# A fused decoder layer on one core: turns, scores and values grouped in even slots, adaLN products moved

## The chip, the core and the metric

The kernel runs on one core of a Trainium2 chip. The metric is the device time of one execution in microseconds (us), the median of several runs. The engines are TensorE (PE, and PEld for its weight loads), VectorE (DVE), ScalarE (ACT), GpSimd (POOL) and SyncE (SP), which issues the transfers. Each engine works through its own list of instructions in order; semaphores tie them together.

## The reference

One layer of a hybrid decoder for a prompt of 512 tokens and 8 single sample tokens, width 1024, 8 + 8 heads of 64:

```
mod = silu(c) @ w_ada + b_ada                      # 6 x 1024 numbers: shift, scale, gate, twice
h   = rms_norm(x, g_norm1) * (1 + scale1) + shift1
z   = h @ w_in                                     # q, k, v of mixers A and B, indexer, gates
A   : index scores -> top 128 keys -> softmax(q k - alibi) v
B   : softmax(q k + forget sums) v
x  += gate1 * ((sigmoid(ga) * (A @ w_o_a) + sigmoid(gb) * (B @ w_o_b)) @ w_out)
x  += gate2 * (relu(h2 @ w_up)^2 @ w_down)         # h2 from norm 2, shift2, scale2
```

The sample tokens do the same against paged caches of 256 rows.

## The kernel before

Projections are products in which both the weights and the input are split into a high and a low part: `half_tile` does three products per chunk of 128 inputs (hi x hi, lines 976; hi x lo, 977; lo x hi, 978), for one half of the columns (256 or 264 of the 520). A half tile over all 8 chunks is 24 products, over 4 chunks 12. ScalarE rounds the weights (`round_w`, line 1499), GpSimd or VectorE makes the rest (`rest_w`).

The stretch that the change touches is the loop over `ITERATIONS`: steps p = 0 to 9 with slots s = 0 to 7. Every engine goes through the same (p, s) list with its own work for each, and this fixes the order. Step p projects the q, k, v of head pair p (slots 0 to 3 one half tile of 24 products each, slots 4 to 7 half of one, 12 products), and does the attention of pair p - 1, in 8 units: U = 8 (p - 1) + s. A unit is one head and one block of 128 queries; block qb = 0 to 3 sees (qb + 1) x 128 keys. In step 0 index scores (line 1128) stand in that place. Its work for a unit:

- `scores(U)`, at even U for two heads at once: products of 64 rows, into banks 4 and 5 (L1064);
- `logits(U)` on VectorE adds the mask or forget sums and takes the maximum, `exps(U)` on ScalarE (L1550), `inverse_sum(U)` on VectorE and `probs(U)` on ScalarE (L1556) a slot later;
- `turn_probs(U)`: qb + 1 transpositions into bank 6 (L1073), at slot U + 2, and `store_pt(U)` on ScalarE copies them out (L1563);
- `values(U)` for two heads, products of 64 columns into bank 7 (L1087), at slot U + 5;
- `round_o` on ScalarE and `rest_o` on VectorE (L2095) split the finished output of a pair, in slots 3 and 4.

The projected q and k go through `to_tokens` (four transpositions into bank 2, L1105), `square_tok` (ScalarE), `mean_squares` (VectorE, L2072, L2073), `power` (GpSimd, L829), `normalize` (VectorE, L2082) and `to_features` (four transpositions into bank 3, L1118), for q at slots 2 to 4 and for k at slots 4 to 6; `store_back` takes them out of bank 3.

Two kinds of other work lie in the same slots. `side_step` prepares the samples (list `SIDE`), alternately in banks 2 and 3; ScalarE's `side_store` empties the bank in the slot after. The adaLN products: the last 8 blocks of 512 columns of `w_ada` are each done in two halves, at the 16 places of `ADA_AT`. `mod_part(h)` does one half, 8 products of 32 columns into bank 3 (L1043), `mod_rows_part` (ScalarE, L1606) copies the block out, `mod_turn_part` (L1049) brings it to features by multiplying with `fold_p`, a matrix that also adds the four partial sums, and `mod_add_part` (VectorE) adds the bias. The weights come by `load_part(h)`, issued by SyncE in the slot after half h - 2, when that is done. `mod_part` of an even h waits until the block before is added, and until the side work of earlier steps has left bank 3:

```
            elif h % 2 == 0:
                pe.wait_ge(mod_ready, ADA_BLOCKS + h // 2)
                pe.wait_ge(back_read, 2 * p)
                before = sum(at[0] < p for at in SIDE)
                if before:
                    pe.wait_ge(side_read, before)
```

After the loop come the last gates, the output projections and the MLP.

Of the kernel before, what the change touches and what calls it, by code (L numbers as in the profile page):

```python
# [15 lines left out]
ALU = mybir.AluOpType  # L16
ACT = mybir.ActivationFunctionType
F32 = mybir.dt.float32
# [4 lines left out]
P = 128  # L23
# [37 lines left out]
SPL = 2  # L61
ADA_BLOCKS = 4
ADA_ORDER = [0, 2, 1, 3] + list(range(4, 12))
ADA_AT = [(p, s) for p in range(6) for s in range(0 if p in (1, 4) else 2, 4)]
N_H = NCH + 2
KEPT = list(range(T_WO + NCH + SPL, T_MLP)) + [T_MLP + 2, T_MLP + 3]
N_KEPT = NCH - SPL
# [39 lines left out]
def split_at(p, s):  # L107

    q, t = slot_before(p, s)
    return [T_PAIR + 3 * q + HALVES_AT.index(t) // 2 + SPL] if 0 <= q <= N_PAIRS + 1 and t in HALVES_AT[1::2] else []  # L110
# [36 lines left out]
def layer(nc, a):  # L147
    ctx = ExitStack()
    with ctx:
# [7 lines left out]
        def sb(name, shape, dt=F32, at=None):  # L157
            size = int(np.prod(shape[1:])) * 4
            size += -size % 32
            if at is None:  # L160
                at = place["at"]
                place["at"] += size
            return nc.alloc_sbuf_tensor_at(name, list(shape), dt, offset=at), at, at + size

        def new(name, shape, dt=F32):
            return sb(name, shape, dt)[0]
# [18 lines left out]
        rs8 = new("rs8", [P, 8])  # L185
        neghalf = new("neghalf", [P, 8])
        sm_tok_s = new("sm_tok_s", [NS, P])
        page_row = new("page_row", [1, NS * NPAGE], I32)

        x_t = new("x_t", [P, NCH, T])  # L190
# [111 lines left out]
        rs_all = sb("rs_all", [P, T], F32, h_hi_at + 4 * T * 4)[0]  # L302
        mod_row, _, e1 = sb("mod_row", [P, 2, SEQ], F32, ts_at)
        cond_p, _, e2 = sb("cond_p", [P, NCH, 32], F32, ts_at + 2048)
        fold_p, _, e2 = sb("fold_p", [P, 9], F32, e2)
        assert e2 <= e1
        part = [sb(f"part{j}", [P, 2, SEQ], F32, at)[0] for j, at in enumerate((pad_at, padb_at, padb_at + 4096, e1))]
        nrm0, _, e1 = sb("nrm0", [P, 2, SEQ], F32, e1)
# [188 lines left out]
            return (qb + 1) * P  # L497


        ITERATIONS = [(p, s) for p in range(N_PAIRS + 1) for s in range(SLOTS)] + [(N_PAIRS + 1, s) for s in range(5)]  # L500
        N_UNITS = N_PAIRS * 2 * QB
        SAMPLE_POWERS = [(5, 7), (6, 1), (8, 2), (8, 4)]
        K_BACK = 6
# [257 lines left out]
        def _(pool):  # L761
# [57 lines left out]
            pool.wait_ge(gq_consts, 1)  # L819
            pool.wait_ge(h_hi_ready, N_H)  # L820
            pool.wait_ge(h_lo_ready, N_H)
            pool.tensor_copy(cond_p[:, :, :], cond_t[:, :, :])
            pool.tensor_copy(fold_p[:, :], fold[:, :]).then_inc(cond_kept, 1)

            def power(n):
                pool.wait_ge(ms_tok, n + 1)
# [51 lines left out]
        def _(pe):  # L878
# [167 lines left out]
            def mod_turn_part(n):  # L1046
                pe.wait_ge(mod_row_ready, ADA_BLOCKS + n + 1)
                for q in range(4):
                    last = mm(bank[3][:, 9 * q:9 * q + 9], mod_row[:, 0, q * P:(q + 1) * P], fold_p[:, :], start=True, stop=True)  # L1049
                last.then_inc(mod_turned, 1)  # L1050

            def unit(U):
# [127 lines left out]

            for p, s in ITERATIONS:
                U = SLOTS * (p - 1) + s
                if s < 4:
                    project(T_PAIR + 3 * p + HALVES_AT.index(s) // 2, HALVES_AT.index(s) % 2)
                elif p <= N_PAIRS:
                    if s in FIRST_HALF_AT:
                        project(T_PAIR + 3 * p + 2, FIRST_HALF_AT.index(s), range(4))
                    else:
                        project(T_PAIR + 3 * p + 2, HALVES_AT.index(s) % 2, range(4, NCH))
                if (p, s) in ADA_AT:  # L1190
                    mod_part(ADA_AT.index((p, s)))
                if p < N_PAIRS:
                    if s == 2:
                        to_tokens(p, 0)
                    if s == 4:
                        to_tokens(p, 1)
                        to_features(p, 0)
                    if s == K_BACK:
                        to_features(p, 1)
                if s == 0 and 1 <= p <= N_PAIRS:  # L1200
                    to_tokens(p - 1, 2)
                if p == 0:
                    if s == 0:
                        pe.wait_ge(act_evac, act_evac_value(T_PAIR - 1, 1))
                        pe.wait_ge(sm_ready, 3)
                    for n in range(3 * s + s % 2, 3 * s + 3, 2):
                        index_scores(n)
                if 0 <= U - 2 < N_UNITS:
                    turn_probs(U - 2)
                if 0 <= U < N_UNITS and U % 2 == 0:  # L1210
                    if U == 0:
                        pe.wait_ge(idx_relu, 24)
                    scores(U)
                if 0 <= U - 5 < N_UNITS and U % 2:
                    values(U - 5)
                if (p, s) == slot_before(*SIDE[4]):
                    first_samples(p)
                if (p, s) in SIDE:
                    side_step(SIDE.index((p, s)))
                if (p, s) in ADA_AT[1::2]:  # L1220
                    mod_turn_part(ADA_AT.index((p, s)) // 2)
# [193 lines left out]
        def _(act):  # L1415
# [229 lines left out]

            for p, s in ITERATIONS:
                U = SLOTS * (p - 1) + s
                before = slot_before(p, s)
                if before in SIDE:
                    side_store(SIDE.index(before))  # L1650
                for i in split_at(p, s):
                    round_w(i)
                if s in HALVES_AT and (p, s) < (N_PAIRS + 1, 4):
                    kd, half = divmod(HALVES_AT.index(s), 2)
                    if p < N_PAIRS:
                        store_z(p, kd, half)
                    else:
                        store_gate(3 * (p - N_PAIRS) + kd, half)
                if p < N_PAIRS and s in (2, 4):
                    square_tok(p, s // 2 - 1)  # L1660
                if (p, s) in ADA_AT[1::2]:
                    mod_rows_part(ADA_AT.index((p, s)) // 2)
                if p == 0:
                    for n in range(3 * s, 3 * s + 3):
                        relu_scores(n)
                if 0 <= U - 2 < N_UNITS:
                    store_pt(U - 2)
                if 0 <= U - 1 < N_UNITS:
                    probs(U - 1)
                if 0 <= U < N_UNITS:  # L1670
                    exps(U)
                if s == 3 and p >= 2:
                    round_o(p - 2)
                if p < N_PAIRS:
                    if s == 4:
                        store_back(p, 0)
                    if s == K_BACK:
                        store_back(p, 1)
                if s == 0 and 1 <= p <= N_PAIRS:
                    store_v(p - 1)  # L1680

# [141 lines left out]
        def _(dve):  # L1823
# [75 lines left out]
            def mod_add_part(n):  # L1899
                at = slice(4 * ADA_ORDER[ADA_BLOCKS + n], 4 * ADA_ORDER[ADA_BLOCKS + n] + 4)  # L1900
                dve.wait_ge(mod_turned, ADA_BLOCKS + n + 1)
                dve.tensor_tensor(mod_t[:, at, :], bank[3][:, 0:36].rearrange("p (q c) -> p q c", c=9),
                                  vec_t[:, at].unsqueeze(2).to_broadcast([P, 4, 9]), ALU.add).then_inc(mod_ready, 1)

            def rest_h(src, j, value):
# [300 lines left out]
            for p, s in ITERATIONS:  # L2206
# [14 lines left out]
                    dve.wait_ge(masks_made, 2 * p)  # L2221
                if 0 <= U - 1 < N_UNITS:
                    inverse_sum(U - 1)
                if s == 4 and p >= 2:
                    rest_o(p - 2)
                if p < N_PAIRS:
                    if s in (2, 4):
# [284 lines left out]
```

## Time and profile before

| | |
|---|---|
| median of 3 runs | 942.34 us (941.03 to 943.38) |
| profiled execution | 939.24 us, span of its instructions 937.4 us |
| TensorE busy | 919.6 us, 98% of the span |
| VectorE, ScalarE, GpSimd busy | 493.9, 396.2, 141.0 us |
| granted TensorE clock | 1.00 |
| chain that ended last | 88% TensorE, 5% VectorE, 4% issue, 2% ScalarE |
| steps 1 to 8 of the loop | from 105.7 to 372 us |

A busy share of TensorE counts pipelined instructions from start to end, so it overlaps: two products that start 0.12 us apart last 0.28 us each. Start times tell more than durations. Slot (3, 1) means step 3, slot 1. "Idle before" is the time in which an engine had nothing under way, with the instruction that ended it.

### The profile page before, as it was taken

To read this page: it belongs to the slowest core of one execution; us is meant where nothing else is said; L and a number is where in the kernel's file an instruction comes from. 1 tells how busy PE (TensorE), PEld (TensorE's weight loads), DVE (VectorE), ACT (ScalarE), POOL (GpSimd) and SP (SyncE) were. 2 spreads that over 40 slices of the span, in tenths; PEclk is the share of its full clock that TensorE was granted. 3 is DMA by queue.
4 is the path that set the end of the run, shared out by engine and by line. 5 is a ranking of instruction groups with operands and counts; after the bars stand their busy time and mean duration, and the time that the engine had idled before them with its cause. 6 is when DMAs were issued, how large, how long until landed. Compare 5 with 4: busy or idle time off the path is not lost.

```text
span 937.4 us, 19878 instructions
## 1 busy us (share of the span) xinstructions
PE 919.6 (98%) x7554; PEld 847.5 (90%) x7554; DVE 493.9 (53%) x1178; ACT 396.2 (42%) x829; POOL 141.0 (15%) x140
## 2 busy tenths in 40 slices
PE   8999999999999999999999999999999999999997
PEld 7797678777878878998999999999999999999997
DVE  3654778864645797731277576444333344443332
ACT  3354646654756667233334244333111244431121
POOL 4200233232236674300000000000000000000000
PEclk9999999999999999999999999999999999999999
DMA  9648765256325554977233431233333333333312
GB/s 319 219 117 235 188 214 174 71 169 193 110 64 158 163 183 131 279 251 249 69 91 97 129 90 47 69 92 94 98 96 91 90 90 89 89 89 90 89 45 92
DMA packets 176233, 124.54 MB, mean 133 GB/s; under 512 B 14739, under 2 KB 152019, under 8 KB 176164
## 3 DMA queue, kind: packets, MB, share of 16 engines
q1 hardware_dynamic: 176034, 123.50, 43.6%
q8 instruction: 45, 0.74, 0.3%
q14 instruction: 24, 0.20, 0.1%
q10 hardware_dynamic: 130, 0.10, 0.0%
HBM read 116.99 MB, written 6.59 MB: 132 GB/s over the span
## 4 chain that ended last, share of the span: by engine, by line
PE 88%; DVE 5%; issue 4%; ACT 2%; POOL 1%; POOLq 0%; ACTq 0%; DVEq 0%
PE bank L976 24%; PE bank L977 23%; PE bank L978 23%; PE bank L1064 2%; PE bank L1087 2%; PE bank L1043 2%; PE bank L882 2%; PE bank L1073 2%; PE bank L1105 1%; PE bank L1261 1%; PE bank L900 1%; PE bank L1049 1%; PE bank L1128 1%; DVE sel L2027 1%; PE bank L1118 1%
## 5 line engine op out<-in xcount | busy, mean ns | idle before, releaser
L976 PE MATMUL bank<-h_hi,w_hi 128*128 128x256 f32 (+1 forms) x1232 | 357.5, 290 | 1.2 <-issue 0.6
L977 PE MATMUL bank<-h_lo,w_hi 128*128 128x256 f32 (+1 forms) x1232 | 348.0, 282 | 0.0
L978 PE MATMUL bank<-h_hi,w_lo 128*128 128x256 f32 (+1 forms) x1232 | 347.5, 282 | 0.0
L976 PEld LDWEIGHTS bank<-h_hi,w_hi 128*128 128x128 f32 x1232 | 232.3, 189 | 23.5 <-issue 17.0
L977 PEld LDWEIGHTS bank<-h_lo,w_hi 128*128 128x128 f32 x1232 | 232.1, 188 | 0.0
L978 PEld LDWEIGHTS bank<-h_hi,w_lo 128*128 128x128 f32 x1232 | 231.7, 188 | 0.0
L976 PE MATMUL bank<-u_hi,w_hi 128*128 128x264 f32 (+1 forms) x512 | 145.1, 283 | 0.0
L977 PE MATMUL bank<-u_lo,w_hi 128*128 128x264 f32 (+1 forms) x512 | 144.7, 283 | 0.0
L978 PE MATMUL bank<-u_hi,w_lo 128*128 128x264 f32 (+1 forms) x512 | 144.5, 282 | 0.0
L2444 DVE TENSOR_TENSOR w_lo<-raw,w_hi 128x1024 fp32r<-128x1024 f32 x58 | 71.1, 1225 | 132.9 <-ACT w_hi L1783 132.9
L1783 ACT ACTIVATE w_hi<-raw 128x1024 fp32r<-128x1024 f32 x58 | 61.3, 1056 | 139.8 <-PE bank L978 139.8
L976 PEld LDWEIGHTS bank<-u_hi,w_hi 128*128 128x128 f32 x512 | 96.6, 189 | 0.0
L977 PEld LDWEIGHTS bank<-u_lo,w_hi 128*128 128x128 f32 x512 | 96.4, 188 | 0.0
L978 PEld LDWEIGHTS bank<-u_hi,w_lo 128*128 128x128 f32 x512 | 96.3, 188 | 0.0
L835 POOL TENSOR_TENSOR w_lo<-raw,w_hi 128x1024 fp32r<-128x1024 f32 x27 | 64.6, 2391 | 134.0 <-ACT w_hi L1499 93.0
L1974 DVE TENSOR_TENSOR w_lo<-raw,w_hi 128x1024 fp32r<-128x1024 f32 x32 | 39.3, 1227 | 52.2 <-ACT w_hi L1499 52.1
L1499 ACT ACTIVATE w_hi<-raw 128x1024 fp32r<-128x1024 f32 x59 | 62.2, 1054 | 7.9 <-PE bank L978 7.8
L1790 ACT ACTIVATE u_f<-bank 128x256 f32<-128x256 f32 (+1 forms) x56 | 21.8, 389 | 97.2 <-PE bank L978 92.3
L2453 DVE TENSOR_TENSOR u_f<-u_f 128x256 f32<-128x256 f32 (+1 forms) x56 | 24.0, 429 | 71.2 <-ACT u_f L1790 70.8
L1550 ACT ACTIVATE lg<-lg,stat 128x128 f32<-128x128 f32 (+3 forms) x64 | 35.9, 560 | 33.4 <-DVE stat L2064 33.0
L1556 ACT ACTIVATE lg<-lg,stat 128x128 f32<-128x128 f32 (+3 forms) x64 | 35.9, 561 | 13.3 <-DVE stat L2068 13.3
L976 PE MATMUL bank<-h_hi,kept_hi 128*128 128x256 f32 (+1 forms) x128 | 36.5, 285 | 0.1
(330 smaller groups left out, 1372.2 us busy)
## 6 DMA issues: line engine op xcount, KB each, us to landing
raw<-in_w_in SPq DMA_DIRECT2D x44, 512.0 KB, 4.0
part<-in_w_ada SPq DMA_DIRECT2D x32, 512.0 KB, 5.5
raw<-in_w_up SPq DMA_DIRECT2D x32, 512.0 KB, 4.1
raw<-in_w_down SPq DMA_DIRECT2D x32, 512.0 KB, 4.0
ada<-in_w_ada SPq DMA_DIRECT2D x4, 2048.0 KB, 13.6
kv<-in_cache_k_b SPq DMA_DIRECT2D x16, 256.0 KB, 4.1
qbc<-q_d SPq DMA_DIRECT2D x16, 256.0 KB, 4.6
kv<-in_cache_k_a SPq DMA_DIRECT2D x16, 256.0 KB, 4.5
```

Of the source, the lines that this page charges most:

```text
L835: pool.tensor_tensor(parts(i)[1], raw[:, i % RAW], parts(i)[0].bitcast(F32), ALU.subtract).then_inc(lo_ready, 1)
L976: mm(out, hi[:, k, :], x_h, start=first and k == ks[0], stop=False)
L977: mm(out, hi[:, k, :], x_l, start=False, stop=False)
L978: end = mm(out, lo[:, k, :], x_h, start=False, stop=last and k == ks[-1])
L1499: A(parts(i)[0], raw[:, i % RAW], ACT.Copy).then_inc(hi_ready, 1)
L1550: A(lg[:, U % 3, 0:w], lg[:, U % 3, 0:w], ACT.Exp, bias=stat[:, 8 + U % 8:9 + U % 8], scale=unit_slope(U), accum_out=stat[:, 16 + U % 8:17 ...
L1556: A(lg[:, U % 3, 0:w], lg[:, U % 3, 0:w], ACT.Copy, scale=stat[:, 26 + U % 2:27 + U % 2]).then_inc(p_ready, 1)
L1783: A(w_hi[:, i % SPL], raw[:, i % RAW], ACT.Copy).then_inc(hi_ready, 1)
L1790: A(u_f[:, 2 * (b % 2) + half, 0:CUT[half + 1] - CUT[half]], half_bank(half + 4 * ((T_MLP + b) % 2), half), ACT.Relu).then_inc(act_evac, 1)
L1974: dve.tensor_tensor(parts(i)[1], raw[:, i % RAW], parts(i)[0].bitcast(F32), ALU.subtract).then_inc(lo_ready, 1)
L2444: dve.tensor_tensor(w_lo[:, i % SPL], raw[:, i % RAW], w_hi[:, i % SPL].bitcast(F32), ALU.subtract).then_inc(lo_ready, 1)
L2453: dve.tensor_tensor(uf, uf, uf, ALU.mult).then_inc(u_sq, 1)
```

## The change

TensorE's odd slots keep the projection and side work alone. In even slots stand, in this order, the turn of the odd unit U - 3, `to_features` (slots 4 and 6), `scores(U)`, `values(U - 6)` and the turn of the even unit U - 2; ScalarE's stores follow that order. `round_o` and `rest_o` come a slot later, and the loop gets one more slot, (9, 5). In steps 2, 3 and 5 the adaLN halves move from slots 2 and 3 to slots 0 and 1. Odd halves come ahead of the projection of their slot. The block is turned by four transpositions instead of products with `fold_p`, and VectorE adds the four partial sums (`tensor_reduce`).

```
-ADA_AT = [(p, s) for p in range(6) for s in range(0 if p in (1, 4) else 2, 4)]
+ADA_AT = [(p, s) for p in range(6) for s in (range(4) if p in (1, 4) else (0, 1) if p else (2, 3))]
...
-                    last = mm(bank[3][:, 9 * q:9 * q + 9], mod_row[:, 0, q * P:(q + 1) * P], fold_p[:, :], start=True, stop=True)
+                    last = tr(bank[3][:, q * P:(q + 1) * P], mod_row[:, 0, q * P:(q + 1) * P], ident[:, :])
...
+                if (p, s) in ADA_AT[1::2]:
+                    mod_part(ADA_AT.index((p, s)))
                 if s < 4:
                     project(T_PAIR + 3 * p + HALVES_AT.index(s) // 2, HALVES_AT.index(s) % 2)
...
-                if (p, s) in ADA_AT:
+                if (p, s) in ADA_AT[0::2]:
                     mod_part(ADA_AT.index((p, s)))
...
-                        to_features(p, 0)
-                    if s == K_BACK:
-                        to_features(p, 1)
...
-                if 0 <= U - 2 < N_UNITS:
-                    turn_probs(U - 2)
-                if 0 <= U < N_UNITS and U % 2 == 0:
-                    if U == 0:
-                        pe.wait_ge(idx_relu, 24)
-                    scores(U)
-                if 0 <= U - 5 < N_UNITS and U % 2:
-                    values(U - 5)
+                if U % 2 == 0:
+                    if 0 <= U - 3 < N_UNITS:
+                        turn_probs(U - 3)
+                    if p < N_PAIRS and s in (4, K_BACK):
+                        to_features(p, s // 2 - 2)
+                    if 0 <= U < N_UNITS:
+                        if U == 0:
+                            pe.wait_ge(idx_relu, 24)
+                        scores(U)
+                    if 0 <= U - 6 < N_UNITS:
+                        values(U - 6)
+                    if 0 <= U - 2 < N_UNITS:
+                        turn_probs(U - 2)
...
+                if (p, s) in ADA_AT[1::2]:
+                    mod_rows_part(ADA_AT.index((p, s)) // 2)
                 for i in split_at(p, s):
                     round_w(i)
...
-                if 0 <= U - 2 < N_UNITS:
+                if U % 2 == 0 and 0 <= U - 3 < N_UNITS:
+                    store_pt(U - 3)
+                if p < N_PAIRS and s in (4, K_BACK):
+                    store_back(p, s // 2 - 2)
+                if U % 2 == 0 and 0 <= U - 2 < N_UNITS:
                     store_pt(U - 2)
...
-                if s == 3 and p >= 2:
+                if s == 4 and p >= 2:
                     round_o(p - 2)
...
+                link(dve.tensor_reduce(mod_sum[:, :, :], bank[3][:, :].rearrange("p (q j c) -> p q c j", q=4, j=4)[:, :, 0:9, :],
+                                       AX_X, ALU.add))
+                dve.tensor_tensor(mod_t[:, at, :], mod_sum[:, :, :],
...
-                if s == 4 and p >= 2:
+                if s == 5 and p >= 2:
                     rest_o(p - 2)
```

## Rows read from the trace of the kernel before

**Rows 1.** Windows: stretch, us; busy us (instructions) by engine; clock, DMA share, GB/s

```profile
core 0: us, PE busy (x) PEld busy (x) DVE busy (x) ACT busy (x) POOL busy (x), PEclk, DMA share, GB/s
130.90:148.00 17.10, 16.41 (x128) 13.69 (x129) 16.45 (x59) 11.16 (x26) 2.51 (x3) 1.00 0.28 82
164.80:183.00 18.20, 17.48 (x136) 14.66 (x136) 17.49 (x58) 11.17 (x26) 2.45 (x3) 1.00 0.25 76
...
105.70:372.00 266.30, 260.57 (x2130) 215.08 (x2129) 184.70 (x597) 167.01 (x412) 106.81 (x52) 1.00 0.49 150
```

**Rows 2.** Timeline of TensorE, steps 6 and 7: start us, us, instruction, idle before

```profile
310.17 0.60 PE L1166 MATMUL bank<-ident,z_s 128*8 128x128 f32 x4
310.52 0.36 PE L976 MATMUL bank<-h_hi,w_hi 128*128 128x256 f32 x1
310.72 0.28 PE L977 MATMUL bank<-h_lo,w_hi 128*128 128x256 f32 x1
...
313.44 0.60 PE L1105 MATMUL bank<-ident,z 128*128 128x128 f32 x4
313.88 0.60 PE L1073 MATMUL bank<-ident,lg 128*128 128x128 f32 x4
314.41 0.49 PE L1064 MATMUL bank<-k_fm,q_fm 64*128 64x128 f32 x4
314.83 0.39 PE L976 MATMUL bank<-h_hi,w_hi 128*128 128x264 f32 x1
315.06 0.28 PE L977 MATMUL bank<-h_lo,w_hi 128*128 128x264 f32 x1
...
317.84 0.60 PE L1073 MATMUL bank<-ident,lg 128*128 128x128 f32 x4
318.37 0.88 PE L1087 MATMUL bank<-p_t,v_tok 128*64 128x128 f32 x12
319.17 0.38 PE L976 MATMUL bank<-h_hi,w_hi 128*128 128x256 f32 x1
319.39 0.28 PE L977 MATMUL bank<-h_lo,w_hi 128*128 128x256 f32 x1
```

**Rows 3.** Timeline of TensorE: an adaLN block is turned, slot (5, 3)

```profile
267.48 1.06 PE L1049 MATMUL bank<-fold_p,mod_row 128*128 128x9 f32 x8
```

**Rows 4.** Timeline of TensorE: index scores behind adaLN products, scores behind turns

```profile
88.44 0.92 PE L1128 MATMUL bank<-ki,q_idx 64*128 64x384 f32 x4
...
300.72 0.92 PE L1064 MATMUL bank<-k_fm,q_fm 64*128 64x384 f32 x4
```

**Rows 5.** What TensorE waited for: us in total, times, longest

```profile
PE bank L1049 <- ACT mod_row L1606: 1.2, 2, 0.7
PE bank L1073 <- ACT lg L1556: 0.8, 1, 0.8
...
PE bank L1154 <- issue: 0.6, 1, 0.6
...
PE bank L1154 <- ACT k_fm L1581: 0.5, 1, 0.5
```

**Rows 6.** Timeline of TensorE, slot (0, 6)

```profile
100.53 0.66 PE L1118 MATMUL bank<-ident,tok 128*128 128x128 f32 x4 [1.25 <-DVE tok L2082]
```

**Rows 7.** Timeline of TensorE: first and third adaLN half of step 1

```profile
108.75 1.07 PE L1043 MATMUL bank<-part,cond_p 128*32 128x512 f32 x8
...
119.56 1.50 PE L1043 MATMUL bank<-part,cond_p 128*32 128x512 f32 x8
```

**Rows 8.** Timeline of ScalarE: the side store at the start of step 3

```profile
178.38 0.58 ACT L1612 ACTIVATE ki_pt<-bank 128x512 f32<-128x512 f32 x1
```

**Rows 9.** Timelines of VectorE and TensorE in step 4: normalize, to_features

```profile
242.00 0.69 DVE L2082 TENSOR_TENSOR tok<-bank,rs 128x512 f32<-128x512 f32 x1
...
243.27 0.60 PE L1118 MATMUL bank<-ident,tok 128*128 128x128 f32 x4
```

**Rows 10.** Timelines of GpSimd and VectorE, slot (7, 4)

```profile
331.21 2.38 POOL L835 TENSOR_TENSOR w_lo<-raw,w_hi 128x1024 fp32r<-128x1024 f32 x1
...
331.52 2.09 DVE L2073 TENSOR_SCALAR ms<-ms 128x8 f32<-128x8 f32 x1
```

More of the change, by code:

```diff
@@ L187, in layer @@
         sm_tok_s = new("sm_tok_s", [NS, P])
+        mod_sum = new("mod_sum", [P, 4, 9])
         page_row = new("page_row", [1, NS * NPAGE], I32)
@@ L304, in layer @@
         cond_p, _, e2 = sb("cond_p", [P, NCH, 32], F32, ts_at + 2048)
-        fold_p, _, e2 = sb("fold_p", [P, 9], F32, e2)
         assert e2 <= e1
@@ L497, in width @@
             return (qb + 1) * P
-        ITERATIONS = [(p, s) for p in range(N_PAIRS + 1) for s in range(SLOTS)] + [(N_PAIRS + 1, s) for s in range(5)]
+        ITERATIONS = [(p, s) for p in range(N_PAIRS + 1) for s in range(SLOTS)] + [(N_PAIRS + 1, s) for s in range(6)]
         N_UNITS = N_PAIRS * 2 * QB
@@ L821, in _ @@
             pool.wait_ge(h_lo_ready, N_H)
-            pool.tensor_copy(cond_p[:, :, :], cond_t[:, :, :])
-            pool.tensor_copy(fold_p[:, :], fold[:, :]).then_inc(cond_kept, 1)
+            pool.tensor_copy(cond_p[:, :, :], cond_t[:, :, :]).then_inc(cond_kept, 1)
             def power(n):
@@ L1660, in _ @@
                     square_tok(p, s // 2 - 1)
-                if (p, s) in ADA_AT[1::2]:
-                    mod_rows_part(ADA_AT.index((p, s)) // 2)
                 if p == 0:
@@ L1671, in _ @@
                     exps(U)
-                if s == 3 and p >= 2:
+                if s == 4 and p >= 2:
                     round_o(p - 2)
[L1674 to L1678, printed above, removed]
                 if s == 0 and 1 <= p <= N_PAIRS:
@@ L1901, in mod_add_part @@
                 dve.wait_ge(mod_turned, ADA_BLOCKS + n + 1)
-                dve.tensor_tensor(mod_t[:, at, :], bank[3][:, 0:36].rearrange("p (q c) -> p q c", c=9),
+                link(dve.tensor_reduce(mod_sum[:, :, :], bank[3][:, :].rearrange("p (q j c) -> p q c j", q=4, j=4)[:, :, 0:9, :],
+                                       AX_X, ALU.add))
+                dve.tensor_tensor(mod_t[:, at, :], mod_sum[:, :, :],
                                   vec_t[:, at].unsqueeze(2).to_broadcast([P, 4, 9]), ALU.add).then_inc(mod_ready, 1)
```

## The prediction

> **What bounds the kernel now.** I read the page first, then the windows by step, the timeline of TensorE for one clean step and one step with adaLN work, the list of what TensorE waited for, and last the timelines of VectorE, ScalarE and GpSimd around those waits. In the pair loop (steps 1 to 8) the reader is to see TensorE busy for 260.6 of 266.3 us at a granted clock of 1.00 [rows 1]. So only some 6 us there are open waits; everything else that can be won on TensorE must come from a denser instruction stream. The two stretches in the same rows say the opposite of another engine: from the middle of step 1 to step 2, and from the middle of step 2 to step 3, VectorE is busy for 16.45 of 17.10 and 17.49 of 18.20 us, 96% both times. There VectorE sets the pace and TensorE waits for what it hands on.
>
> The dense stream is not smooth. The rhythm of the projection is 2.78 us over 23 products, 0.121 each (315.06 to 317.84) [rows 2]. Four transpositions take 0.44 (313.44 to 313.88), 0.11 each. But the four turns that come ahead of scores or of values take 0.53, and the first product of a projection after scores or values takes 0.23 or 0.22 to the next instead of 0.12. A projection that follows transpositions pays nothing: four of them in 0.35 and a first product of 0.20, together 0.55, are 4 x 0.11 + 0.12 within 0.01 [rows 2]. The price stands where full-array work meets the scores (64 rows) or the values (64 columns): about 0.09 on the way in, 0.10 on the way out.
>
> **What the grouping saves on TensorE.** Per pair of slots the order was projection, turns, scores, projection, turns, values. It becomes turns, scores, values, turns, and two projection halves in a row.
> - Out of scores: 27 of the 32 score blocks are followed by a projection now, and will be by values: 27 x 0.10 = 2.7 us. The other 5 are followed by side work.
> - Out of values: 19 of 32 are followed by a projection (the others by side or adaLN work), and will be by turns: 1.9 us.
> - Into values: 32 x 0.09 = 2.9 us, since values will stand behind scores, if scores to values costs nothing of its own. The trace has no such pair. The nearest is the index scores straight behind the adaLN products: a block 64x384 lasts 0.92 there, and 0.92 behind turns [rows 4], so the switch is paid once however it is entered. I take 0; the other end is a full price of 0.10 x 32 = 3.2 us less gain. The Trainium skill (TensorE: Matmul & The Clock Gate, Part 3, The mechanism) says that a weight load overlaps running products only if their row groups differ; scores and values share rows, so by that rule the 3.2 would be lost. No row here shows that pair.
> - adaLN: each of 8 blocks is turned by 8 products in 1.06 us [rows 3] and will be by 4 transpositions in 0.60 [rows 2]: 8 x 0.46 = 3.7. The switch behind them, 0.08 x 8 = 0.6, goes; the odd half pays 0.05 more, because it goes straight into a projection: -0.4. Together 3.9.
>
> Sum 11.4 us. VectorE gets one small reduction (144 numbers a partition) for each of the 8 blocks, in the slot after a projection half; I cost it at nothing, hidden by TensorE's next half of 24 x 0.121 = 2.9 us. Without that cover it could not be worth more than one pass of 512 columns each, 0.69 [rows 9].
>
> **Waits that go.** The waits for the adaLN row (1.2), for a turn at (3, 1) (0.8) and before the side transpositions at (1, 7) and (2, 7) (0.6 and 0.5) [rows 5] have their cause removed: the odd half comes a projection earlier, the turn at an odd slot is gone, and store_back comes ahead of the exponentials. In step 0 the 1.25 us before to_features [rows 6] is covered by index scores that now come first. That is 4.3 us of idle time; each of the six costs some 0.14 more, because work that is resumed starts with an emptied pipeline (four transpositions last 0.60, but what follows starts after 0.44 [rows 2]): 5.1 us.
>
> **Waits that come.** Here the change takes back.
> - Loads of w_ada in step 1. Of the four half blocks the third lasts 1.50 instead of 1.07: its weights are not there at once. They are asked for when the first is done, and that stays. From the end of the first (109.8) to the start of the third (119.6) lie 9.8 us [rows 7], afterwards 8.2 (two projection halves of 2.9, the second half block 1.0, transpositions and scores 1.4). So the wait grows from 0.4 to 2.0. The same for the fourth block, whose loads queue behind a store of v: I put 1.6. Together 3.2 us: step 1 gains nothing up to its middle.
> - Side stores. mod_part in slot 0 of steps 2, 3 and 5 must wait until bank 3 is emptied by the side_store of slot 7, and that stands on ScalarE behind the exponential of slot 7, which waits for VectorE. In step 3 that store ends at 178.96 [rows 8], about when the projection of (3, 0) was over; adaLN work came two slots later and never saw this. VectorE's chain is full, and rest_o (one pass of 512 columns, nearest row 0.69 [rows 9]) moves into it, from a slot where it was hidden. TensorE gets there up to 1.3 us earlier, the store comes 0.7 later: 2.0 us. Step 2 the same without rest_o but with all of the time saved before: 2.0. Step 5, where VectorE has slack, 0.4. Together 4.4.
> - to_features and scores of slot 6. rest_o now stands between inverse_sum and normalize in slot 5, and waits for round_o, which ScalarE does behind the exponential of slot 4, itself behind the second turn. In step 4 normalize ends at 242.69 and to_features starts at 243.27 [rows 9]: 0.58 to spare. The chain grows by 0.69 and about 0.7 of waiting for round_o, TensorE comes 0.4 later: 0.2 of wait, and logits in front of the next scores bring it to 0.6 to 1.0. If the mean's small operation meets GpSimd's rest_w it gets worse: 8 columns took 2.09 us and ended with GpSimd's pass (331.21 + 2.38) [rows 10]. I put 0.6, 0.7, 1.0, 1.0, 0.5, 0.5, 0.5, 0.4 for steps 1 to 8: 5.2 us. The Trainium skill (SBUF - State Buffer, two separate sides) calls the pair of ports that these two share an exclusive lock, held for the whole instruction; this row agrees (2.09 us).
>
> Sum 12.8 us.
>
> **The total.** -11.4 - 5.1 + 12.8 = -3.7 us. The profiled execution took 939.24 us (span 937.4); 935.5 after. The median is 942.34, so 938.6 by the median. All terms lie in steps 0 to 8; nothing behind them is touched, except that values(62), round_o and rest_o come a slot later, ahead of a projection that needs neither.
>
> **Rivals.**
> 1. The stream gain arrives and the new waits are no more than those that go: -9 to -14, 928 to 933. For it: VectorE and ScalarE are far from full in steps 3 to 8, and each turn gets a slot more of time. Against it: 96% in the two stretches [rows 1].
> 2. The gain is used up: within 0.3% (2.8 us, about what a measurement of this kernel can tell from no change). The dense blocks pay the full switch from scores to values (+3.2) and one of the waits is 1 us longer: 942.
> 3. Slower, by one mechanism: two turns in one slot share bank 6, so the second waits for ScalarE's store of the first. At slot 0 some 1.0 us of scores and values lie between them, and a store of 512 columns takes 0.58 [rows 8]: 0.4 to spare, if ScalarE is free. But in even slots it has side_store, round_w, store_z and square_tok ahead of it. If it is late by 0.7, 0.3 us is lost in each of 32 even slots: 9.6 us, 948. It decides from 0.2 per slot on. Against it: ScalarE is busy for 167 of 266 us [rows 1], and the store has 1.4 to 2.3 us in slots 2 and 4.
>
> **How the numbers follow.** My forecast (a net of -1.5 to -7) 0.50, rival 1 0.20, rival 2 0.20, rival 3 0.10. Its own range is 935 to 941. Over 0.3% faster: rival 1 and four fifths of the forecast, 0.60; within: 0.30; slower: 0.10. The range for 8 in 10 leaves out the far half of rivals 1 and 3: 931 to 944.
>
> **What would show it.** First products of a projection at 0.20 and no 0.23; projection runs of 36 and 48 products; L1049's successor as four transpositions behind a projection, without idle time. New idle time of TensorE before the adaLN products in (1, 2), (1, 3), (2, 0), (3, 0), named for DMA part or ScalarE; before to_features and scores in slot 6, named for VectorE; none before the second turn. If scores to values shows an extra 0.1, the first term is 3 us too large. The prediction is wrong if the adaLN products of (2, 0) and (3, 0) start without a wait, or if idle time stands before the second turn in most even slots.

## The result: no gain, 3.4 us more instead of 3.7 us less

| | before | changed kernel |
|---|---|---|
| median | 942.13 us (20 runs, 938.72 to 945.32) | 945.51 us (20 runs, 938.77 to 949.68) |
| profiled execution | 939.24 us, span 937.4 | 949.04 us, span 947.2 |
| TensorE, VectorE, ScalarE, GpSimd busy | 919.6, 493.9, 396.2, 141.0 us | 917.9, 503.6, 394.3, 138.8 us |
| granted TensorE clock, mean of the profiled execution | 1.000 | .992 |
| chain that ended last | 88% TensorE | 75% TensorE, 8% VectorE, 7% issue, 3% SyncE's queue, 3% ScalarE, 2% DMA |

The ratio is 1.0032 with a 95% interval of [1.0018, 1.0046]: slower by a little over 0.3%, outside the predicted range of 931 to 944. What first strikes the eye is the spread: 10.9 us between the fastest and the slowest run, against 6.6 before. The 20 runs lie roughly in the order of their mean granted clock: the two at .998 and .999 took 938.8 and 940.6 us, the eight at .992 or less 946.2 to 949.7. The profiled execution is 3.5 us above its median, the one before 2.9 us below its own; the account below is made in the time of these two, 9.8 us apart, and is larger than the medians' 3.4 for that reason.

The windows of the changed kernel, the loop first, answer to [rows 1].

```profile
core 0: us, PE busy (x) PEld busy (x) DVE busy (x) ACT busy (x) POOL busy (x), PEclk, DMA share, GB/s
105.70:382.00 276.30, 258.34 (x2108) 212.80 (x2106) 194.93 (x606) 166.54 (x415) 106.33 (x52) 0.98 0.47 145
118.00:128.00 10.00, 6.84 (x33) 2.36 (x31) 1.23 (x5) 1.55 (x4) 2.44 (x2) 0.83 1.01 325
146.00:157.00 11.00, 8.73 (x61) 6.67 (x59) 8.74 (x31) 6.01 (x14) 2.06 (x1) 0.84 0.22 72
```

The loop needs 10.0 us more than its 266.3 us, TensorE's busy time in it is 2 us less (although it holds 5 us that a lower clock adds, see below), so its open waits grew from 6 to 18 us. In two short stretches, steps 1 and 2, the clock is .83 and .84; in the first of them the DMA engines are full (share 1.01). The list of what TensorE waited for from 105 to 375 us says what the waits are (us in total, times, longest); it answers to [rows 5].

```profile
PE bank L1117 <- DVE tok L2086: 4.4, 6, 1.7
PE bank L1042 <- ACT ki_pt L1615: 3.7, 2, 2.3
PE bank L1042 <- DMA part<-in_w_ada: 3.2, 1, 3.2
PE bank L1117 <- DVE mod_t L1906: 2.7, 1, 2.7
PE bank L1072 <- ACT p_t L1566: 1.3, 1, 1.3
PE bank L1063 <- DVE stat L2068: 1.1, 4, 0.3
PE bank L1042 <- ACT srow L1619: 0.6, 1, 0.6
```

(L1117 is `to_features`, L1042 the adaLN products, L1072 the turns, L1063 the scores; `ki_pt` and `srow` are what side stores write.) Of the waits that were to go, the five in [rows 5] and the one in [rows 6] are gone; a shorter one at (0, 4) grew from 0.5 to 0.9 us. The timeline of TensorE at the first of the new ones, slots (1, 2) and (1, 3), answers to [rows 7]:

```profile
118.47 0.28 PE L977 MATMUL bank<-h_hi,w_lo 128*128 128x256 f32 x1
121.91 3.08 PE L1042 MATMUL bank<-part,cond_p 128*32 128x512 f32 x8 [3.16 <-DMA part<-in_w_ada]
124.92 1.12 PE L1104 MATMUL bank<-ident,z 128*128 128x128 f32 x4
125.97 0.76 PE L1063 MATMUL bank<-k_fm,q_fm 64*128 64x256 f32 x4
...
126.92 1.06 PE L1042 MATMUL bank<-part,cond_p 128*32 128x512 f32 x8
```

Two things are to be seen. The wait is 3.16 us; TensorE is there at 118.7. And the eight products behind it last 3.08 us, the eight of (1, 3) 1.06: they run at the lower of TensorE's two clocks. Windows laid over the three such stretches of the loop, each behind one of the waits of 3.16, 2.74 and 2.27 us, show 0.50, that is 1.2 GHz instead of 2.4:

```profile
122.70:126.10 3.40, 3.40 (x12) 1.04 (x10) 0.00 (x0) 0.03 (x1) 0.00 (x0) 0.50 0.99 324
136.40:139.80 3.40, 3.40 (x13) 2.00 (x12) 1.32 (x7) 1.06 (x3) 1.64 (x1) 0.50 0.56 154
153.40:156.80 3.40, 3.40 (x17) 1.68 (x11) 1.59 (x4) 0.92 (x3) 1.85 (x1) 0.50 0.32 113
```

A stretch of 3.4 us at half the clock does 1.7 us of work less, so each of these waits costs half as much again and more. A fourth such stretch, in the prologue at 23.7 us, does not come from the change: eleven of the fourteen traces have it, that of kernel 12 below too, which leaves the kernel before as it is but for the places of two adaLN halves. With it, and with a start that was 0.7 us later already, this execution is 0.6 us behind the one of before at the scores of (1, 0); one below without it (kernel 6) is 1.9 us ahead there.

When the weights were asked for stands in SyncE's own timeline, first in the changed kernel, then before:

```profile
111.11 0.33 SPq L618 DMA_DIRECT2D lfp<-in_cache_logf_b  x1
113.49 1.32 SPq L600 DMA_DIRECT2D part<-in_w_ada  x2
...
112.55 1.10 SPq L600 DMA_DIRECT2D part<-in_w_ada  x2
```

The first half ends at 110.4 us. SyncE is still at the transfers of the index pages until 111.4, issues four more, and asks for the third half's weights at 113.49, 3.1 us behind the end of the first (before: 2.7 us behind it). Then the two loads take 8.6 us to land (median), before 6.2. The chain that ended last runs through SyncE's list from 80.7 us to this issue and on through the load: that is the 3% of SyncE's queue in the table. Why the loads take longer is not shown; in the other traces that have them at this place they take 6.8 to 8.7.

The second new wait, at (1, 4), is for the addition of an adaLN block. The timelines of VectorE and GpSimd:

```profile
133.96 0.31 DVE L1904 TENSOR_REDUCE mod_sum<-bank 128x36 f32<-128x144 f32 x1
134.30 1.77 DVE L1906 TENSOR_TENSOR mod_t<-mod_sum,vec_t 128x36 f32<-128x36 f32 x1
...
133.68 2.34 POOL L834 TENSOR_TENSOR w_lo<-raw,w_hi 128x1024 fp32r<-128x1024 f32 x1 [4.37 <-ACT w_hi L1502]
```

The addition of 36 numbers lasts 1.77 us and ends with GpSimd's pass (133.68 + 2.34 = 136.02); in the seven other blocks it lasts 0.20. It also starts late, behind a whole top round of VectorE. `to_features` waits 2.74 us for it.

The denser stream itself is all there. The timeline of TensorE at slot (7, 2), to be read beside [rows 2]:

```profile
322.83 0.49 PE L1072 MATMUL bank<-ident,lg 128*128 128x128 f32 x3
323.25 0.49 PE L1063 MATMUL bank<-k_fm,q_fm 64*128 64x128 f32 x4
323.67 0.66 PE L1086 MATMUL bank<-p_t,v_tok 128*64 128x128 f32 x8
324.26 0.66 PE L1072 MATMUL bank<-ident,lg 128*128 128x128 f32 x4
324.67 0.37 PE L975 MATMUL bank<-h_hi,w_hi 128*128 128x264 f32 x1
324.88 0.28 PE L976 MATMUL bank<-h_lo,w_hi 128*128 128x264 f32 x1
```

The scores take 0.42 to the next instruction, as before the projection in [rows 2]; the eight values behind them 0.59, and twelve in the next even slot 0.81, as the twelve of [rows 2] (318.37 to 319.17 is 0.80). From scores to values nothing extra is paid. Four turns in front of the projection take 0.41 instead of 0.53, its first product 0.21 instead of 0.23, and 48 products follow without a switch.

### The profile page after: what moved, and what is told of

Its sections match the earlier page's. It is cut to its first block, busy times and chain, and to the rows that moved or that the text cites. A ratio compares the mean times of both kernels' runs of the same rounds, so it can differ in the third digit from the quotient of the medians.

```text
span 947.2 us, 19821 instructions
## 1 busy us (share of the span) xinstructions
PE 917.9 (97%) x7522; PEld 844.8 (89%) x7522; DVE 503.6 (53%) x1186; ACT 394.3 (42%) x829; POOL 138.8 (15%) x139
## 4 chain that ended last, share of the span: by engine, by line
PE 75%; DVE 8%; issue 7%; SPq 3%; ACT 3%; DMA 2%; POOL 1%; POOLq 0%; ACTq 0%; DVEq 0%
PE bank L975 21%; PE bank L976 21%; PE bank L977 21%; PE bank L881 2%; SPq L616 2%; PE bank L1042 1%; PE bank L1063 1%; PE bank L1072 1%; DVE sel L2031 1%; PE bank L1086 1%; PE bank L899 1%; DMA part<-in_w_ada 1%; PE bank L1264 1%; DVE lg L2063 1%; PE bank L1104 1%
## 5 line engine op out<-in xcount | busy, mean ns | idle before, releaser
L1566 ACT ACTIVATE p_t<-bank 128x128 f32<-128x128 f32 (+3 forms) x64 | 27.7, 433 | 37.6 <-PE bank L1072 37.5
## 6 DMA issues: line engine op xcount, KB each, us to landing
ada<-in_w_ada SPq DMA_DIRECT2D x4, 2048.0 KB, 13.5
```

The lines of the kernel that those rows point to most:

```text
L1566: A(p_t[:, qb % 2, hh, 0:qb + 1, :], bank[6][:, 0:width(qb)].rearrange("p (k c) -> p k c", k=qb + 1), ACT.Copy).then_inc(pt_ready, 1)
```

## The experiments

Kernel 1 is the kernel of experiment 1, and so on. Each was timed in five rounds beside the kernel before, on one chip for each group of four: 12 runs each, but 7 of kernel 1 and 6 of kernel 8. Ratios are to the kernel before; two whose difference is under some 0.2% are not told apart.

| kernel | median, us | before, us | ratio, 95% interval |
|---|---|---|---|
| changed kernel | 945.51 | 942.13 | 1.0032 [1.0018, 1.0046] |
| 1 grouping only | 946.95 | 941.54 | 1.0047 [1.0025, 1.0069] |
| 2 adaLN changes only | 944.23 | 941.54 | 1.0029 [1.0014, 1.0045] |
| 3 sum in PSUM | 944.16 | 941.54 | 1.0022 [1.0007, 1.0037] |
| 4 halves at slots 2, 3 | 944.89 | 941.54 | 1.0030 [1.0013, 1.0047] |
| 5 halves from step 1 to 5 | 939.69 | 942.60 | 0.9971 [0.9958, 0.9984] |
| 6 rest_o last | 945.40 | 942.60 | 1.0028 [1.0012, 1.0044] |
| 7 turned by products | 945.59 | 942.60 | 1.0033 [1.0018, 1.0048] |
| 8 three fixes | 937.58 | 942.60 | 0.9950 [0.9932, 0.9968] |
| 9 the same adaLN, no grouping | 941.27 | 941.53 | 0.9991 [0.9973, 1.0009] |
| 10 filler in the wait | 943.86 | 941.53 | 1.0021 [1.0005, 1.0037] |
| 11 three fixes, rounds deferred | 938.07 | 941.53 | 0.9958 [0.9941, 0.9975] |
| 12 before, halves from step 1 to 5 | 940.46 | 941.53 | 0.9996 [0.9980, 1.0012] |

**1. Only the grouping**: the adaLN lines as before.

```
-ADA_AT = [... (range(4) if p in (1, 4) else (0, 1) if p else (2, 3))]
+ADA_AT = [... range(0 if p in (1, 4) else 2, 4)]
...     # mod_part behind the projection, rows behind square_tok, turned with fold_p, no reduction
```

> The grouping of turns, scores and values alone; the adaLN halves stand, are turned and are added as in the kernel before. Theory 1 (the loss comes from the adaLN moves, the grouping is sound): the switches between projection and attention save 7 to 8 us on TensorE, the waits of slot 6 give back 3 to 5, the waits at (1, 7), (2, 7), (0, 6) and (3, 1) go: 4 to 8 us faster than the kernel before, no wait above 1 us before adaLN products in steps 2 and 3, granted clock near 1.00. Theory 2 (the grouping itself is what costs, because ScalarE and VectorE get their work in bursts): within 1 us of the changed kernel, so 2 to 5 us slower than the kernel before.

It has the highest ratio of all, 1.0047, though its interval meets that of the changed kernel. What TensorE waited for:

```profile
PE bank L1050 <- ACT mod_row L1609: 5.0, 7, 0.7
PE bank L1074 <- ACT p_t L1566: 3.4, 3, 1.9
PE bank L1119 <- DVE tok L2084: 3.0, 7, 1.2
```

Before, turns and values stood between an adaLN half and the turning of its block; the grouping takes them out of the odd slots, and now seven of the eight blocks wait 0.7 us each for ScalarE's copy (before: two, 1.2 us together [rows 5]). So the grouping alone can't have its gain; by this list it needs the odd halves ahead of the projection, which is the other part of the change. My first theory missed this. The time of theory 2 came out, 4.4 us slower, and 3.4 us of its cause is in the list too, the turns that wait for ScalarE; but the largest item is neither theory's.

**2. Only the adaLN changes**: the kernel before with all of the new adaLN lines, turns, scores and values as before.

> The adaLN changes alone (places, odd halves ahead of the projection, transpositions, the sum on VectorE); turns, scores and values as in the kernel before. Theory 1: the waits that the changed kernel shows in (1, 2), (1, 4) and (2, 0) are here too, so 3 to 8 us slower than the kernel before, with a granted clock below 1.00 in most executions. Theory 2: 3 to 4 us faster, the saving of four transpositions against eight products and of two waits for the adaLN row.

1.0029: the loss is there without any grouping. It has the waits for w_ada (1.4 us), for the side store (1.3) and for the addition (0.4), all shorter than in the changed kernel, where TensorE arrives earlier.

**3. The sum kept in PSUM**, so that the addition has one operand there.

```
+                mod_psum = bank[3][:, :].rearrange("p (q c) -> p q c", q=4)[:, :, 16:25]
-                link(dve.tensor_reduce(mod_sum[:, :, :], ...))
-                dve.tensor_tensor(mod_t[:, at, :], mod_sum[:, :, :],
+                link(dve.tensor_reduce(mod_psum, ...))
+                dve.tensor_tensor(mod_t[:, at, :], mod_psum,
```

> The changed kernel, but the sum over the four partial rows is written to unused columns of bank 3 and the bias is added from there, so that the addition has one operand in SBUF and not two. Theory 1 (the addition waited for GpSimd's rest_w because both inputs lay in SBUF): it takes about 0.2 us in (1, 4) in place of 1.77, TensorE's wait before to_features there falls from 2.74 to about 1.1 us, and the clock has a dip less: 1.5 to 3 us faster than the changed kernel. Theory 2 (the addition was slow for another reason, or the wait is filled by the next one): less than 0.7 us.

The additions of all blocks by duration (least, median, most, ns), in the changed kernel and here:

```profile
L1906 DVE TENSOR_TENSOR mod_t<-mod_sum,vec_t x8: 195/196/1772, 94.6 to 269.2; 128x36 f32<-128x36 f32 x8
```

```profile
L1907 DVE TENSOR_TENSOR mod_t<-bank,vec_t x8: 194/195/196, 95.0 to 266.1; 128x36 f32<-128x36 f32 x8
```

That it was GpSimd's pass which made the addition long is shown here, since the addition of (1, 3) again starts inside one (timelines of GpSimd and VectorE):

```profile
134.72 2.35 POOL L834 TENSOR_TENSOR w_lo<-raw,w_hi 128x1024 fp32r<-128x1024 f32 x1 [4.37 <-ACT w_hi L1502]
...
135.34 0.20 DVE L1907 TENSOR_TENSOR mod_t<-bank,vec_t 128x36 f32<-128x36 f32 x1
```

The long addition is gone, and the wait for mod_t falls from 2.7 to 1.2 us; in this execution the wait for w_ada was 3.9 us. The time falls by 0.1%, which the intervals don't separate from nothing.

**4. The halves of steps 2, 3 and 5 back at slots 2 and 3**, the rest as changed.

> The changed kernel with the adaLN halves of steps 2, 3 and 5 back in slots 2 and 3; odd halves still ahead of the projection. Theory 1 (bank 3 is freed late behind the exponential of slot 7): the waits before the adaLN products of (2, 0), (3, 0) and (5, 0), 2.3 + 1.5 + 0.6 us idle, are gone, those of slot 2 are under 0.3 us; the wait of step 1 stays; 2 to 5 us faster than the changed kernel. Theory 2 (VectorE's full chain sets the time of these stretches, and the wait only moves): another wait of about the same size before turns or scores in slots 0 to 2 of steps 2 and 3, and under 1 us of gain.

1.0030, as the changed kernel. The waits for the side store (3.7 us) are gone, and waits for the store of the turned probabilities rise from 1.3 to 5.1:

```profile
PE bank L1072 <- ACT p_t L1566: 5.1, 4, 1.9
PE bank L1042 <- DMA part<-in_w_ada: 3.1, 1, 3.1
...
PE bank L1117 <- DVE mod_t L1906: 2.6, 1, 2.6
```

ScalarE is late in slot 0 of steps 2 and 3 whichever of its stores TensorE asks for first. The wait changes its name, not its length.

**5. Two of step 1's four halves moved to step 5.**

```
-ADA_AT = [... (range(4) if p in (1, 4) else (0, 1) if p else (2, 3))]
+ADA_AT = [... (range(4) if p in (4, 5) else (0, 1) if p else (2, 3))]
```

> The changed kernel with step 1's second pair of half blocks moved to step 5 (halves at (1, 0), (1, 1) and at (5, 0) to (5, 3)). Theory 1, the loads: TensorE's wait of 3.2 us for part at 118.5 us, the half clock behind it and the wait of 2.7 us at 133.2 for the addition all stand in step 1 and go with the crowd there; 3 to 5 us shorter than the changed kernel (945.5), so 941 to 943, and the granted clock rises by .002 to .004. Theory 2, a clock that falls wherever it will: 945 or more, and as many stretches at 0.5 as before.

0.9971: 5.7 us less than the changed kernel (1.0032 - 0.9971 = 0.0061 of 942; by the two intervals some 1.8 us more or less), and faster than before. It is the one edit that turns the sign. The same stretch as above, slots (1, 2) to (1, 3), and then what TensorE waited for in the loop:

```profile
118.00:128.00 10.00, 8.95 (x70) 7.53 (x69) 7.45 (x28) 5.58 (x16) 4.73 (x3) 1.00 0.86 290
```

```profile
PE bank L1117 <- DVE tok L2086: 6.3, 7, 2.0
PE bank L1072 <- ACT p_t L1566: 2.5, 3, 1.1
PE bank L1063 <- DVE stat L2068: 1.9, 5, 0.8
```

70 products instead of 33 start in these 10 us, at full clock. No wait for w_ada, for mod_t or for ki_pt is left. At the scores of (1, 4) this execution is 11.1 us ahead of the changed kernel's; some 2.5 us of that is work that comes back in step 5. At the scores of (1, 6) it is 9.3 ahead, since VectorE's normalize is now what comes last there, and in (1, 7) 6.4, behind a stretch at half clock; at the scores of (2, 0) it is 10.2 ahead again, because the changed kernel waits 2.3 us for a side store there, at half clock behind it, and this one does not. So the gain holds a side store's wait too. The spread of the runs shrinks from 10.9 us to 3.5 (937.6 to 941.1). The granted clock did not rise (median of the runs .9935, changed kernel .9955): the stretches at half clock now stand behind a wait of 2.0 us at (1, 6), 6.8 us of it, and one of 1.7 at (2, 6), 3.4 us, in sum as long as the changed kernel's three. That half of my expectation was wrong, so the gain is in the waits and not in fewer such stretches.

**6. rest_o behind normalize and logits** in slot 5 of VectorE.

> The changed kernel with rest_o behind normalize and logits in slot 5 of VectorE. Theory 1: the chain that to_features and scores of slot 6 wait for gets shorter by 0.7 us and the wait for round_o leaves it; the waits there in steps 2 to 8 (some 5 us of idle time together in the profiled execution) fall under 2: 942 to 943.5. Theory 2: that chain was not the limit, or the 0.7 us only moves to logits of slot 6: within 1 us of 945.5.

1.0028, not told apart from the changed kernel. In the trace the waits for tok fall from 4.4 us (6 times) to 2.4 (twice), as theory 1 says, but those for the side store and for the turned probabilities are 1.7 us longer (4.3, 1.2 and 1.8 against 3.7, 0.6 and 1.3). Theory 2 holds for the time.

**7. The block turned by products with fold_p again**, without the reduction.

> The changed kernel with the adaLN row turned by the products with fold_p, as before, so no reduction on VectorE. TensorE pays 8 x 0.46 = 3.7 us more. Theory 1, the reduction and the addition from SBUF (1.77 us at 133) are a side cost: 1 to 2 us come back at (1, 4), so 946 to 948. Theory 2, VectorE's new work is what lost the time: at least 4 us come back, 945 or less.

1.0033, the same as with the transpositions, though TensorE's stream carries 3.7 us more. The long addition is gone with the reduction, and TensorE, later, waits 1.7 us for w_ada at (1, 2) instead of 3.2; the eight products behind that wait still last 2.98 us, at half clock. In this placement the transpositions are worth nothing: what they save is waited away.

**8. Three fixes together**: the halves of step 1 to step 5 and those of steps 2, 3 at slots 1 and 2; the sum in PSUM; rest_o last.

```
+ADA_AT = [... (range(4) if p in (4, 5) else (2, 3) if p == 0 else (0, 1) if p == 1 else (1, 2))]
```

> The changed kernel with the halves of step 1 thinned out to step 5, those of steps 2, 3 and 5 at slots 1, 2, the sum kept in PSUM, and rest_o behind logits. Theory 1, the loss is made of these waits and of the half clock behind the long ones: the 11 us of the stream stay as a net gain of 3 to 6 us against the kernel before (941.5), so 935.5 to 938.5, at a granted clock of .998 or more. Theory 2, the grouping has a price of its own (a wait in each even slot, or a clock that falls anyway): 940 or more.

0.9950, 4.7 us faster than before, and 7.7 us faster than the change as it was made. Its waits:

```profile
PE bank L1072 <- ACT p_t L1566: 6.1, 5, 1.8
PE bank L1117 <- DVE tok L2087: 4.4, 3, 2.1
PE bank L1042 <- ACT srow L1619: 0.8, 1, 0.8
```

The wait that is left over is rival 3's: the second turn of an even slot, behind ScalarE. At (3, 0), timelines of TensorE and ScalarE:

```profile
177.68 0.66 PE L1086 MATMUL bank<-p_t,v_tok 128*64 128x128 f32 x8
180.12 0.63 PE L1072 MATMUL bank<-ident,lg 128*128 128x128 f32 x4 [1.78 <-ACT p_t L1566]
...
177.80 0.58 ACT L1615 ACTIVATE ki_pt<-bank 128x512 f32<-128x512 f32 x1
178.28 1.04 ACT L1502 ACTIVATE w_hi<-raw 128x1024 fp32r<-128x1024 f32 x1
179.22 0.37 ACT L1532 ACTIVATE z<-bank 128x256 f32<-128x256 f32 x1
179.49 0.49 ACT L1566 ACTIVATE p_t<-bank 128x384 f32<-128x384 f32 x1
```

The side store, a weight rounding and the store of z lie in front of the first store of probabilities, as the rival says.

**9. The adaLN part of kernel 8 without the grouping**: the kernel before with the new adaLN lines, the sum in PSUM and kernel 8's places.

> The kernel before (nothing grouped) with the adaLN changes as the kernel with the three fixes has them: odd halves ahead, turned by transpositions, the sum in PSUM, halves thinned out of step 1. Theory 1, the grouping earns its 7.5 us of stream and pays some 4 of them back in waits of slots 0 and 6: this kernel is 3 to 4 us slower than the one with the three fixes (937.6), so 940.5 to 942. Theory 2, the grouping is worth nothing and all of the gain is adaLN's: 936.5 to 938.5.

0.9991. So the grouping (with `rest_o` at its place in kernel 8) is worth 0.4% (0.9991 - 0.9950), some 4 us, with these fixes, out of 7.5 us of stream. Theory 1 holds.

**10. A filler in the wait**: 24 transpositions of a constant ahead of the adaLN products of (1, 2), overwritten by them.

```
+                if ADA_AT[h] == (1, 2):
+                    for _ in range(24):
+                        tr(bank[3][:, 0:P], ident[:, :], ident[:, :])
```

> The changed kernel with 24 idle transpositions of ident (24 x 0.11 = 2.6 us) ahead of the adaLN products of (1, 2), in the time in which TensorE waits for part (3.2 us in the profiled execution). Theory 1, the half clock behind that wait is granted because TensorE stood still: the eight products behind it last 1.0 us instead of 3.0, with no stretch at 0.5 there, and the time falls by 2 us, to 943.5. Theory 2, the clock falls there whatever TensorE does: the products still last 2 us or more, 945.5 or above.

The timeline of TensorE:

```profile
118.46 2.78 PE L1040 MATMUL bank<-ident 128*128 128x128 f32 x24
121.72 1.05 PE L1045 MATMUL bank<-part,cond_p 128*32 128x512 f32 x4 [0.48 <-DMA part<-in_w_ada]
123.00 1.05 PE L1045 MATMUL bank<-part,cond_p 128*32 128x512 f32 x4 [0.22 <-DMA part<-in_w_ada]
...
125.46 1.93 PE L1045 MATMUL bank<-part,cond_p 128*32 128x512 f32 x8
```

The weights come no earlier (121.7 against 121.9), but the scores and the turn behind the products are done at 125.5 instead of 126.9, and from 118 to 140 us the granted clock is 1.00 where the changed kernel has .84. The clock follows what TensorE did before: busy with useless work it stays at full rate. The addition of (1, 3) starts at 132.90 here, just ahead of GpSimd's pass at 132.95, and lasts 0.20 us; the wait for it is 0.4. The filler has thus moved both of the troubles at (1, 4) away in this execution. The time is 1.0021, 1.0 us below the changed kernel by the ratios and 1.7 by the medians; the direction is as expected, the size is not resolved.

**11. Kernel 8 with the top rounds of slots 4 and 6 a slot later**, behind the logits.

> The kernel with the three fixes (937.6), with the top rounds of slots 4 and 6 of steps 1 and 2 behind logits of slots 5 and 7. Theory 1, VectorE's order is what TensorE waits for there: the waits of 2.1 us at (1, 6) and 1.1 at (2, 6) fall under 0.5, those of ScalarE's store at (2, 0) and (3, 0) (1.0 and 1.8) shrink too, and the half clock at 133 us goes: 3 to 5 us less, 933 to 935. Theory 2, VectorE is full and the same work only moves its wait to slots 0 and 2: within 1 us of 937.6.

0.9958, as kernel 8. The waits for tok fall from 4.4 to 2.0 us, and 1.5 us of issue, 0.5 for z_s and 0.6 more for ScalarE appear. In steps 1 and 2 VectorE is full (28.8 us of 30 in kernel 8 from 120 to 150 us); another order only moves its lateness. Theory 2 holds.

**12. The kernel before with two halves from step 1 to step 5.**

> The kernel before with step 1's second pair of adaLN half blocks moved to step 5, nothing else. Theory 1, before had slack enough in step 1 (0.4 us of wait for part): within 1 us of before. Theory 2, the crowd in step 1 cost it too, and thinning it out is a gain of its own: 2 us or more faster than before, 939.5 or less.

0.9996: nothing. (Here slots 0 and 1 of step 1 lose their halves, in kernel 5 slots 2 and 3.) The crowd in step 1 cost the kernel before nothing that can be measured. It costs only where TensorE comes early.

## Why the prediction failed, step by step

- **The stream, -11.4 us: right.** Each price stands in the rows as computed, scores to values at nothing; the other end of 3.2 us (the Trainium skill's rule, TensorE: Matmul & The Clock Gate, Part 3, The mechanism, would have given it) is not seen: twelve values take 0.81 us behind scores and 0.80 behind turns.
- **Waits that go: right**, but for 0.4 us at (0, 4).
- **"Loads of w_ada in step 1 ... Together 3.2 us": this step failed.** As priced, 1.6 us more of wait for the third half and 1.6 for the fourth. It rested on "They are asked for when the first is done, and that stays". Neither trace shows that: SyncE's list came between, before with a weight load that waited for GpSimd (2.7 us), in the changed kernel with page transfers (3.1 us), and the third half's loads then took 8.6 us to land where those of before took 6.2. So the third waited 3.2 us (I had 2.0); the fourth did not wait. In place of its 1.6 stood the addition, 2.7 us. Moving the second pair of halves away, by my sum worth these 3.2 us, was worth 5.7 (kernel 5), the side store of (2, 0) included.
- **"I cost it at nothing, hidden by TensorE's next half": failed with it.** The reduction is 0.31 us, but the addition behind it reads two operands from SBUF and once met GpSimd's pass (1.77 us instead of 0.20), and both stand behind a top round on a VectorE that I had myself shown at 96%. I looked at the reduction's length and not at where it would stand in VectorE's list. I had even named the row for such a meeting [rows 10] and applied it to another instruction. The same page of the Trainium skill that I cited (SBUF - State Buffer, two separate sides) names VectorE's operations with two SBUF inputs against GpSimd's as the case; with PSUM as one input the eight additions of kernel 3 last 0.19 to 0.20 us, as it says, the one that starts inside GpSimd's pass too. In time this is small: kernel 3 gains 0.1%, kernel 7 nothing.
- **The clock: left out altogether.** The sum was made at a clock of 1.00. Of the three waits of over 2 us in the loop I had forecast two myself, at 2.0 us each; all three were followed by 3.4 us at half clock, 1.7 us each. The trace of before had no such row, but the runs of that kernel beside the experiments have mean clocks from .993 to 1.000, with medians of .997 and .998, so it meets such stretches as well and the two profiled executions overstate the difference. By the medians (.9955 against .997 to .998) the clock adds 1.4 to 2.4 us, an estimate. The Trainium skill (TensorE: Matmul & The Clock Gate, Part 1) says that a wait for loads can drop the clock; the trace agrees behind the wait for w_ada. Kernel 10 shows for this wait, in one execution, that it is TensorE's standing still that does it.
- **Side stores, 4.4 us: right**, 2.3 + 1.5 + 0.6 = 4.4. They are not the loss, though: kernel 4 takes the first two away and ScalarE makes TensorE wait elsewhere.
- **Slot 6, 5.2 us: near**, a little too large. The list has 4.4 + 1.1, and 0.8 more comes behind it, at (8, 6): 6.3 us; but 2.3 of these waits stood in the trace of before already (1.97 at (7, 6)), which my sum did not set off. So 4.0 are new. `rest_o` was their cause in part (kernel 6), without effect on the time.
- **The restart behind a wait:** the sum gave 0.14 us back for each wait that goes and charged nothing for those that come. By the traces 14 have come in the loop, 2.0 us at that price.
- **Rival 3, the second turn**: 1.3 us in one slot of 32, not 0.3 in each. It becomes the largest wait only in kernel 8.

In the profiled executions: stretches at half clock 5.1 us in the loop and 1.7 in the prologue, a start 0.7 later ahead of that, the addition 2.7, the loads -0.4 against my price, the second turn 1.3, slot 6 -1.2, the wait at (0, 4) 0.4, the restarts 2.0: 12.3 of the 13.5 us between my -3.7 and the +9.8. The 2.4 us of the prologue are not the change's.

In the median the gap is 7.1 us. Kernel 5 puts the crowd in step 1 at 5.7 us where my sum had it at 3.2: that is 2.5 us of the gap, 1.8 more or less. The rest, over 4 us, stays in kernel 5 too, which my sum would have at -6.9 us and which came out at -2.7; the lower clock of its runs (.9935 against .997) is worth 3.3 us of that, an estimate, and no run was made without these stretches, so this part stays open. How the crowd's 5.7 us divide between the late weights, the late addition and the clock behind them the runs don't tell: kernel 3, which takes the long addition away, and kernel 10, which fills the wait, gain 0.9 and 1.0 us and are hardly told apart from nothing. That each, taken alone, leaves the next one to end last is my reading; kernels 4 and 6 show such a shift for other waits. I had given "slower" a chance of 0.10, for the mechanism of rival 3, and that one cost 1.3 us; the time came out slower by others.

## What to carry to other kernels

A denser stream on the bounding engine is worth what its suppliers can follow: ask which load, copy or sum was on time by a few tenths and price it after the saving has moved the consumer forward, all in one place, not one by one. When a load is asked for is read from the list of the engine that issues it, not from the event that allows it. Work that has free choice of its place (here the adaLN halves) belongs out of the stretch in which the other engines are full; moving two of them was worth more than any other single fix. A wait of some 2 us on TensorE should be priced with the half clock that may follow it, and the price is a chance, not a certainty.

## What the runs showed of the hardware

- TensorE fell to 0.50 for 3.4 us (6.8 once each in kernels 5 and 12) behind many of its waits, not all. In the loop, over all fourteen traces: behind all 4 waits of 3.1 to 3.9 us, 3 of 4 of 2.6 to 2.7 (the one of 2.58 in kernel 9 was not followed), 4 of 5 of 2.3, 9 of 12 of 1.9 to 2.1, 3 of 9 of 1.7 to 1.8, and none of 1.5 us or less. In the prologue the same wait of 1.40 us was followed by such a stretch in 11 of the 14. What decides is open. Useless transpositions in the wait kept the clock at 1.00 (kernel 10, one execution).
- The changed kernel spread over 10.9 us in 20 runs, kernel 5 over 3.5 in 12. The wait for w_ada does not explain this by itself: kernels 3 and 4, which have it, spread over 6.7, and the kernel before, where no such wait is seen, over 6.6 to 8.6. The cause was not measured.
- An addition of 36 numbers on VectorE, 0.20 us, lasts to the end of GpSimd's pass when both its operands are in SBUF and it starts inside that pass: 1.77 us in the changed kernel, 1.85 and 1.82 in kernels 4 and 6. With one operand in PSUM it started inside such a pass five times (before and kernels 1, 3, 7, 12) and took 0.20. Started 0.05 and 0.15 us ahead of the pass (kernels 10 and 2) it took 0.20 also with both operands in SBUF.
